# A decoder step with fp32 products in three matmuls: order of the vector work around the down projection

## The reference

```python
D_MODEL, D_FF, CONV_W = 1024, 2816, 3
def conv_ffn(x, conv_prev, w_up, conv_w, conv_b, w_down):
    u = x @ w_up                                   # (T, 2 * D_FF)
    ue = jnp.concatenate([conv_prev, u], 1)
    c = conv_b
    for j in range(CONV_W):
        c = c + ue[:, j:j + T] * conv_w[j]         # causal, depthwise
    a, b = jnp.split(c, 2, axis=-1)
    return (jax.nn.silu(a) * b) @ w_down, ue[:, -(CONV_W - 1):]
...
x = layer_norm(DN_ALPHA * x + f, ln_ffn_g, ln_ffn_b)
```

## Time and profile before

| | us |
|---|---|
| median of 3 runs | 2974.15 (2973.24 to 2974.48) |
| the profiled execution | 2971.17 |
| its span in the trace | 2969.4 |
| PE busy in the span | 2771.0 (93%) |
| DVE, ACT, POOL busy | 1975.8, 1266.5, 1140.7 |

### The profile page before, as it was taken

One profiled execution on the slowest core, in us unless ns is written; L12 is line 12 of the kernel. 1 busy time (PEld: TensorE's weight loads), 2 busy tenths in 40 slices (PEclk: granted clock), 3 DMA queues, 4 the chain that ended last, 5 costly groups with the idle time before them and its releaser, 6 DMA issues. The chain is left out here.

```text
span 2969.4 us, 46576 instructions
## 1 busy us (share of the span) xinstructions
PE 2771.0 (93%) x16663; PEld 2455.0 (83%) x16663; DVE 1975.8 (67%) x3107; ACT 1266.5 (43%) x2588; POOL 1140.7 (38%) x963
## 2 busy tenths in 40 slices
PE   8898899999998999998997998998998999998995
PEld 7455678887898999996875898997898999997874
DVE  3466644667576777768888563445576777768888
ACT  5344542334353444444444564334353444444433
POOL 1245321112245565554446001212145556554435
PEclk9999899999999999999998999999999999999997
DMA  3100440103212222235542011113212122235542
GB/s 116 51 8 13 150 159 19 54 23 125 81 50 107 90 78 105 89 139 175 184 129 100 24 37 42 41 37 125 78 53 105 74 95 103 75 136 190 183 129 82
DMA packets 125700, 271.26 MB, mean 91 GB/s; under 512 B 24330, under 2 KB 41627, under 8 KB 124500
## 3 DMA queue, kind: packets, MB, share of 16 engines
q1 hardware_dynamic: 125556, 269.35, 26.6%
HBM read 202.15 MB, written 67.81 MB: 91 GB/s over the span
## 5 line engine op out<-in xcount | busy, mean ns | idle before, releaser
L136 PE MATMUL psum<-xT_hi,tk_w 128*128 128x320 f32 (+1 forms) x1536 | 457.0, 298 | 23.0 <-DVE tk_u L3128 17.7
L138 PE MATMUL psum<-xT_hi,tk_w 128*128 128x320 f32 (+1 forms) x1536 | 456.6, 297 | 0.0
L137 PE MATMUL psum<-xT_lo,tk_w 128*128 128x320 f32 (+1 forms) x1536 | 455.4, 296 | 0.0
L136 PEld LDWEIGHTS psum<-xT_hi,tk_w 128*128 128x128 f32 x1536 | 292.3, 190 | 24.3 <-issue 21.3
L137 PEld LDWEIGHTS psum<-xT_lo,tk_w 128*128 128x128 f32 x1536 | 292.7, 191 | 0.0
L136 PE MATMUL psum<-tk_operands 128*128 128x512 f32 x616 | 246.8, 401 | 48.5 <-DVE x_or_mix L3226 27.8
L138 PEld LDWEIGHTS psum<-xT_hi,tk_w 128*128 128x128 f32 x1536 | 291.6, 190 | 0.0
L136 PE MATMUL psum<-tk_t,tk_w 128*128 128x256 f32 x960 | 283.8, 296 | 3.6 <-POOL tk_w L2426 2.1
L138 PE MATMUL psum<-tk_t,tk_w 128*128 128x256 f32 x960 | 283.8, 296 | 0.0
L137 PE MATMUL psum<-tk_t,tk_w 128*128 128x256 f32 x960 | 283.1, 295 | 0.0
L2426 POOL TENSOR_TENSOR tk_w<-tk_sums,tk_w 128x512 fp32r<-128x512 f32 x160 | 233.6, 1470 | 116.4 <-ACT tk_w L2751 116.4
(11 more groups left out here) (486 smaller groups left out, 7236.1 us busy)
## 6 DMA issues: line engine op xcount, KB each, us to landing
tk_wraw<-in_w_up SPq DMA_DIRECT2D x88, 512.0 KB, 4.0
tk_graw<-ates_between_projections SPq DMA_DIRECT2D x88, 320.0 KB, 4.0
ates_between_projections<-tk_c SPq DMA_DIRECT2D x44, 512.0 KB, 3.2
tk_graw<-ates_between_projections SPq DMA_DIRECT2D x66, 256.0 KB, 2.7
tk_draw_xT<-in_w_down SPq DMA_DIRECT2D x32, 512.0 KB, 6.4
ates_between_projections<-tk_g SPq DMA_DIRECT2D x22, 576.0 KB, 4.5
x_between_sublayers<-x_or_mix SPq DMA_DIRECT2D x18, 512.0 KB, 2.6
tk_resid<-x_between_sublayers SPq DMA_DIRECT2D x18, 512.0 KB, 3.9
```

The costliest lines, as they stand in the source:

```text
L136: nc.tensor.matmul(out, a[0], b[0], start=first, stop=False, skip_group_check=shared)
L137: nc.tensor.matmul(out, a[0], b[1], start=False, stop=False, skip_group_check=shared)
L138: return nc.tensor.matmul(out, a[1], b[0], start=False, stop=last, skip_group_check=shared)
```

## The change

Seven things, all inside `phase_trunk` but for one buffer offset:
1. The gates and the sample of a step lie in one operand `gx` of 2×640, split by one ACT and one DVE instruction in place of two each. Weights get buffers of their own (`bx`, `early`).
2. The weight sums are not issued with the step that uses them: M7's (and M4's in group 1) are made during M1, M6's during M3, M4's of group 0 during M6, M5's during M2.
3. The last chunk's convolution is spread over M2 and M5 of group 0, its gate stands after step (0, M5, 4), directly ahead of the takes of M5; ACT's silu and copy move along.
4. SP issues the raw weights of chunk 3 ahead of the store of chunk 1's gates, and 18 gate loads ahead of the last `store_odd` in place of three.
5. In `window(2)` the four weight sums of chunk 3 come after the three `plus`, not between them.
6. In the final norm POOL adds the bias of tiles 1 and 2 (DVE before); the statistics of tile 4 stand behind M7's takes and its `rstd` in the tail.
7. Buffers that had to make room move (`halves`, `nraw`, `swa_skip`).

```diff
@@ buffers
-    wx = [m.at(f"{tag}operands{k}", PLACES[k], [P, 2, 2, 512], R) for k in range(6)]
...
+    gx = [m.at(f"{tag}g_operand{k}", (16384, 21504, 26624, 60416, 65536, 31744)[k], [P, 2, 640], R) for k in range(6)]
+    bx = [m.at(f"{tag}d_operand{k}", (81920, 86016, 70656, 74752, 45056, 49152, 12288)[k], [P, 2, 512], R) for k in range(7)]
...
+    SUMS_IN = lambda g, i: {M3: (M6,), M1: (M7, M4) if g else (M7,), M6: () if g else (M4,)}.get(i, ())
...
-    by_dve = lambda n: n in WHOLE or 1 <= n < 5
+    by_dve = lambda n: n in WHOLE or n in (3, 4)
@@ PE and d_hi: where a step's weights lie
+    def d_split(g, i, k):
+
+        return early[:, 2 * (k - 4):2 * (k - 4) + 2, 512:D] if g == 0 and i in (M2, M5) and k >= 4 else bx[6 if g and k == 4 else k][:]
@@ SP
             store_even(0, 0)
+            next_raw(2)
             store_odd(1, 0)
-            next_raw(2)
...
-            for n in range(6, 9):
+            for n in range(6, 24):
                 load_g(n)
             store_odd(LAST, 10)
-            for n in range(9, 12):
-                load_g(n)
@@ POOL
-                if (g, i) == (1, M7) and k in (2, 3):
-                    fnorm.scale(pool, k - 1)
-            for n in range(3, NT - len(WHOLE)):
+                if (g, i, k) == (1, M7, 3):
+                    fnorm.scale(pool, 1)
+                    fnorm.add_bias(pool, nc.gpsimd, 1)
+            for n in range(2, NT - len(WHOLE)):
                 fnorm.scale(pool, n)
@@ ACT, g_hi and d_hi
-                last = nc.scalar.activation(wx[k][:, 0, 0, :], graw[n % 6][:, at:at + 512], ACT.Copy)
-                if i in WITH_SAMPLE:
...
-                    last = nc.scalar.activation(gs[k][:, 0, :], graw[n % 6][:, at:at + P], ACT.Copy)
-                last.then_inc(ah, 1)
+                wide = P * tiles_of(i)
+                nc.scalar.activation(gx[k][:, 0, 0:wide], graw[n % 6][:, 0:wide], ACT.Copy).then_inc(ah, 1)
...
+                if n in (2, 3):
+                    act.wait_ge(pr, END + 12)
...
-                    act.wait_ge(ts, summed_steps(n))
...
+                    act.wait_ge(ts, SUMMED_BY[g, i, k])
+                if (g, i, k) == (1, M2, 4):
+                    act.wait_ge(ste, 32 * 11)
+                if g == 0 and i == M3 and k >= 4:
+                    act.wait_ge(cvd, 2 * NJ)
+                    act.wait_ge(sk, 2 * NJ)
@@ ACT, the loop over the steps
+                if (g, i, k) == (0, M5, 2):
+                    silu(LAST)
+                if (g, i, k) == (0, M5, 5):
+                    copy_g(LAST, 1, 10)
@@ DVE
-            window(2)
+            window(2, ((), (), (), range(4)))
...
-                last = nc.vector.tensor_tensor(wx[k][:, 0, 1, :], graw[n % 6][:, at:at + 512], f32(wx[k][:, 0, 0, :]), ALU.subtract)
...
+                nc.vector.tensor_tensor(gx[k][:, 1, 0:wide], graw[n % 6][:, 0:wide], f32(gx[k][:, 0, 0:wide]), ALU.subtract).then_inc(al, 1)
...
+            LATE_CONV = {(0, M2, 1): (1, 1), (0, M2, 3): (1, 0), (0, M5, 0): (0, 1), (0, M5, 1): (0, 0)}
...
-            conv(LAST, 1, 0)
             g_lo(2)
-            conv(LAST, 0, 1)
-            conv(LAST, 0, 0)
...
-            gate(LAST, 1)
...
-                if n + 1 < LAST_PRODUCT and after(n + 1) is not None:
-                    d_sum(after(n + 1))
...
+                for x in SUMS_IN(g, i):
+                    d_sum(g, x, k)
                 if after(n) is not None:
                     g_lo(after(n))
+                if (g, i, k) in LATE_CONV:
+                    conv(LAST, *LATE_CONV[g, i, k])
+                if (g, i, k) == (0, M5, 4):
+                    gate(LAST, 1)
...
-                    if k:
+                    if 1 <= k < 4:
                         fnorm.rstd(dve, link, k)
-                    if k < 4:
-                        dve.wait_ge(ad, TAKEN[1, M6, k])
-                        fnorm.stats(dve, link, k + 1)
+                    if k != 3:
+                        dve.wait_ge(ad, TAKEN[1, M6, min(k, 3)])
+                        fnorm.stats(dve, link, min(k, 3) + 1)
...
-            for x, biases in enumerate(((1, 2), (3,), (4,), ())):
+            for x, biases in enumerate(((), (3,), (4,), ())):
+                if x == 0:
+                    fnorm.rstd(dve, link, 4)
```

## The result

The changed kernel takes **2940.47 us** (median of 4 runs, 2939.17 to 2941.87) against 2974.32 for the kernel before (4 runs): ratio 0.9886, 95% interval 0.9868 to 0.9903, 34 us or 1.1% less. A second set of runs gave 2938.98 and 0.9876 (0.9856 to 0.9895). The forecast was 2943 in a range of 2926 to 2957. The profiled execution took 2941.11 and its span is 2939.3. PE is busy as long as before, 2771.7 us against 2771.0, for the matmuls are the same; its idle time has shrunk by 30.8 us.

What follows compares the result with a forecast made beforehand. PE, busy 2771.0 of 2969.4 us, was taken as the bound, so only its idle or slow time could be won back. Terms 21 + 0 + 0.6 + 10 = 31.6, taken as 31: 2974.15 − 31 = 2943, range 2926 to 2957.

Steps and rivals of the forecast that it cites:

- (a): Start of the up projection: PE's waits for a `plus` of chunk 2 go, with their slow clocks; 21 us, from 15 to 24.
- (d): M7 and the end, group 1: DVE's shorter queue and the tail gain 10 us for both layers, from 0 to 16.
- (b): Takes of M2 and M5, group 0: earlier M2 take offset by a new wait at M5's; 0, from −8 to +13.
- (c): Group 1's wait of 2.8 at 1516.17: 0.3 shorter, slow clock stays; +0.6 us for both layers, 0 to 11.6.
- The rule on the ports: Whoever issues first keeps the ports, so the gate's 1.2 may fall on POOL; whole gain 33 in place of 31.
- rival A: M2's take in time: fewer DVE meetings with POOL remove its remaining wait and clock; 13.4 more, 2930; chance 0.2.
- B: Start of the up projection: PE still waits for POOL's splits, (a) is 11, 10 less; 2953; chance 0.12.
- C: End of group 1: POOL's added biases delay the scales, (d) is 0, 10 less; 2953; chance 0.08.
- D: Sums added in M3, M1 and M6 make waits at 8 product boundaries, 46 us against 31; 2989; chance 0.05.
- (e): What costs nothing: merged sample splits, weight sums moved into M3, M1 and M6, ACT's new waits, SP's gate loads.

Runs made afterwards that it cites:

- second profile: The changed kernel run and profiled again, unchanged, as a measure of scatter; 2938.98 us.
- the kernel with the samples apart: The changed kernel with the gate splits in two instructions again (512 columns and the sample's 128) on ACT and DVE; 2941.56 us.

## Why the prediction was right, point by point

**The sum.** Forecast 31.6 of 21 + 0 + 0.6 + 10; the columns of the first profile give 21.2, −2.9, 7.1 and 11.9, which is 37.3, and −7.3 of scatter. The time is inside the forecast's own narrow range. Two terms are good, (a) and (d); (b) is off by a step of its own sum, and (c) was low, by luck of the clock. That the total came within 3 us is in part luck too: the columns give 5.7 more than forecast, and the scatter of the mixers took 7.3 back.

**The places.** I put all three waits of the down projection at a product's fourth tile. By the trace only the wait for M2's takes is there, in M5; the ones for M5's and M7's takes stand at the very first tile of M3 and of M4, in group 1 too, and the wait of 1.2 is in M2's fourth step. The takes that end them are the ones I named.

**(a), 21, measured 21.2.** The chain of causes was right: SP issued the weights before the stores, DVE's takes no longer waited for them. To compare with the earlier trace rows, take off 5.8 us, by which this execution was behind the one of before when the up projection began: the issue at 895.34 is 889.5 there, where 890.1 was forecast. From the timelines of SP and DVE in the changed kernel:

```profile
895.34 0.80 SPq L2263 DMA_DIRECT2D tk_wraw<-in_w_up  x2
...
899.06 0.69 DVE L3135 TENSOR_TENSOR tk_u<-tk_u,psum 128x512 f32<-128x512 f32 x1
...
903.38 0.68 DVE L3117 TENSOR_TENSOR tk_sums<-tk_wraw 128x512 f32<-128x512 f32 x1
```

What is late next was placed wrong in detail: I charged 1.1 for the chain of chunk 3 on DVE, and PE waits 1.3 there for an ACT instruction (913.46 above). The two edits were treated as one term; the runs split it, and one of them does most of it.

**(b), 0, measured 3.1 + 8.0 − 14.0 = −2.9.** Every step of it is in the trace: the wait of 1.2 gone, M2's take earlier but not early enough, a new wait ahead of M3 with the gate right before the takes. The step that was wrong is in the sum. The take came 5.2 us earlier against the start of M2, for 5.0 forecast: 1357.98 in place of 1367.67 is 9.7, and 4.4 of these was the lead when M2 began. But I added the vanished wait of 1.2 to that. PE resumes when the take is done, so a wait that goes ahead of it only lets PE come sooner and wait longer there: 4.98, not the 3.6 of the forecast. The columns for both places hold 1.5 + 3.8 = 5.3 and 1.6 + 4.2 = 5.8, near the 5.0 and not at 6.2. Without the 1.2 the sum is −1.3 a layer, −2.6 in all, against −2.9.

The take's 5.0 was right with two errors in it that cancel. I priced its two convolutions at 1.35 each from rows where POOL was idle, and both met POOL's splits here; but fewer others did. Of the DVE instructions ahead of this take eight were stretched before; now five are in full, the two convolutions among them, and two in part. DVE and POOL in M2 and M5 of the changed kernel:

```profile
1343.53 5.22 POOL L2478 TENSOR_TENSOR tk_d_operand<-tk_d,tk_d_operand 128x512 fp32r<-128x512 f32 x3 [0.17 <-ACT tk_d_operand L2838]
...
1347.52 2.46 DVE L3075 SCALAR_TENSOR_TENSOR tk_c<-tk_u,tk_cw,tk_c 128x1168 f32<-128x1168 f32 x1
...
1353.05 1.84 POOL L2478 TENSOR_TENSOR tk_d_early<-tk_d,tk_d_early 128x512 fp32r<-128x512 f32 x1
1353.69 2.43 DVE L3078 SCALAR_TENSOR_TENSOR tk_c<-tk_u,tk_cw,tk_c 128x1168 f32<-128x1168 f32 x1
...
1377.19 1.40 POOL L2478 TENSOR_TENSOR tk_d_operand<-tk_draw_xT,tk_d_operand 128x512 fp32r<-128x512 f32 x1 [2.10 <-ACT tk_d_operand L2838]
1377.37 2.46 DVE L3085 TENSOR_TENSOR tk_c<-tk_c 128x1168 f32<-128x1168 f32 x1
...
1379.86 0.69 DVE L3089 TENSOR_TENSOR tk_g<-tk_g,tk_c 128x512 f32<-128x512 f32 x1
...
1380.70 1.70 POOL L2478 TENSOR_TENSOR tk_d_operand<-tk_draw,tk_d_operand 128x512 fp32r<-128x512 f32 x1 [2.11 <-ACT tk_d_operand L2838]
1381.31 1.63 DVE L3093 TENSOR_TENSOR tk_c<-tk_c 128x512 f32<-128x512 f32 x1
...
1382.87 0.68 DVE L3226 COPY x_or_mix<-psum 128x512 f32<-128x512 f32 x1
```

The convolutions take 2.46 and 2.43, some 4.7 for both from start to start in place of 2.7. The gate lasts from 1377.37 to 1382.87, 5.5, where I had 4.7: it met two splits of POOL (2.46 in place of 1.36, 1.63 in place of 0.69), not one. The wait before M3 was 4.42 for 3.8 expected, and 2.8 for the clock in place of 2.5 (less, 1.5 and 1.7, in the second profile). Here the runs add what the sum could not show: the gate's place cost 14.8 us of the whole, and the same gate behind the takes costs nothing.

**The rule on the ports.** My rival A and its neighbour rested on how often DVE and POOL meet. The gate of 1377.37 began 0.18 after POOL's split of 1377.19 and was stretched by 1.1, so there POOL was first; that the 1.2 would fall on POOL is refuted for this place. It agrees with what the Trainium skill states in "SBUF — State Buffer", section "Who interferes with whom", that the first to issue keeps the ports and the other blocks; only who is first can't be told from the order of the code. The same section says that a DVE instruction with at most one SBUF input, outside its 2-port modes, is left alone, and the trace agrees: of five takes from PSUM the first two began inside a split of POOL, and all kept the 0.60 from one to the next that the earlier trace rows shows for four (2.47 there, 3.07 for five here).

```profile
1357.46 1.72 POOL L2478 TENSOR_TENSOR tk_d_early<-tk_d,tk_d_early 128x512 fp32r<-128x512 f32 x1 [2.57 <-ACT tk_d_early L2838]
...
1357.98 0.68 DVE L3226 COPY x_or_mix<-psum 128x512 f32<-128x512 f32 x1
```

**(c), 0.6, measured 7.1.** The wait shortened by 0.64 a layer, 2.82 to 2.18, where 0.3 was expected. What was mis-sized is mainly the clock: I let its 3.0 stand, and in this execution it was full behind the wait in both layers. It is no merit of the change: in the second profile one of the two was slow, and the kernel with the samples apart has the old wait of 2.82 with the full clock.

**(d), 10, measured 11.9.** The steps are in the trace: DVE's stretch between the takes of M6 and M7 fell from 22.7 to 15.4 us (1561.83 to 1577.23), 7.3 less where 6.4 was expected, with DVE now waiting for ACT; then POOL's bias and split hold the last step. DVE and POOL there:

```profile
1567.70 1.69 DVE L3193 TENSOR_TENSOR tk_g_operand<-tk_graw,tk_g_operand 128x512 fp32r<-128x512 f32 x1 [0.94 <-ACT tk_g_operand L2823]
...
1577.23 0.69 DVE L3228 TENSOR_TENSOR x_or_mix<-x_or_mix,psum 128x512 f32<-128x512 f32 x1 [0.25 <-DVE tk_f_negmean L1984]
...
1580.23 2.71 POOL L2011 TENSOR_TENSOR x_or_mix<-x_or_mix,tk_ffn_bias 128x1024 f32<-128x1024 f32 x1
...
1582.89 1.28 POOL L2478 TENSOR_TENSOR tk_d_operand<-tk_draw_xT,tk_d_operand 128x512 fp32r<-128x512 f32 x1
```

But the prices of the parts don't hold one by one. I put the sums at 6.5 a layer; put back alone, four of them lengthen the wait by 1.5 a layer and cost 3.1 in all, because DVE otherwise waits for ACT. The statistics, 1.8 a layer, do lengthen the wait by 2.0, but with the norm's old order around them they cost 0.9 in all.

**The rivals.** A (M2's take in time) didn't come: 5.0 us are left. B (start half) didn't: 21.2. C (nothing at the end) didn't, though POOL does bound the last product's first tile. D (waits at other boundaries) didn't: in M3, M1 and M6 no wait of 0.8 us or more exists in the changed kernel, and the lead over the kernel before stays within 0.1 us from M3 to group 1's wait in both layers. So the sums that moved there cost nothing, as (e) said; the merged splits, also in (e), do gain a little in group 1, as the kernel with the samples apart shows.

## What to carry to other kernels

Lay the n-th matmul of two traces beside each other and read the lead place by place: it resolves 1 us where the program's time scatters by 5. When one wait of an engine stands ahead of another whose end a second engine sets, count only the later end: what the first gives back, the second takes. A queue ahead of a PSUM take is worth clearing of everything that nobody waits for: the same gate costs 7 us a layer ahead of the takes and nothing behind them. When two removals shorten the same queue, don't add their prices; test one at a time and both together.

## What the runs showed of the hardware

Behind equal waits PE's clock differed. These are windows of 4 us behind the wait of 2.19 ahead of M3 in group 1, in the second and (above) the first profile of the same program:

```profile
1509.80:1513.80 4.00, 3.97 (x12) 3.17 (x13) 3.01 (x5) 0.00 (x0) 0.54 (x1) 0.69 0.51 178
```

0.69 here, with 12 matmuls, and 1.00 there, with 18. Over the profiles of this study the wait of 2.2 at this place had the low level behind it 12 times and the full one 10 times, at a price of 1.6 to 1.7 us or 0.1; waits of 3.7 and more in the down projection always had it, at 1.4 to 4.0 (the excess over full speed in the 30 matmul rows behind each, further waits taken out), and waits of up to 1.5 us there never. In between both occur: of the waits for takes, 1.8, 1.9 and once 2.2 at M2 had the full level, 2.1 there and 2.4 at M7 the low one, and 2.8 in group 1 the full one in one kernel and the low one in two, at 1.5 to 3.0. So a wait near 2 us has a price that one profile can't tell, and a forecast should carry both values.
